# Norms by token tile, gains by row and whole first slabs in a two-block transformer on one core

## What is computed

```
h = rmsnorm(x, ln1);  z = h @ w_in                     # q, k, v of three attentions, three gates
merged = sum_b sigmoid(g_b) * (attention_b @ w_p_b);   x = x + merged @ w_o
h2 = rmsnorm(x, ln2); u = conv3(h2 @ w_up);            x = x + (silu(a) * b) @ w_down
x = rmsnorm(x, ln_f)
mem_n = rms_norm(mem, mem_norm_g);  kv = mem_n @ wkv   # 256 memory rows, 2048 columns
p = rms_norm(x, g0) @ w_in_first                       # convolution branch and RWKV branch
x = x + rms_norm(concat(conv, rwkv) @ w_out, g1)
x = x + rms_norm(cross_attention(rms_norm(x, g2) @ wq, kv) @ wo, g3)
x = x + rms_norm(swiglu(rms_norm(x, g4), w_gu, w_down), g5)

rmsnorm(x, g) = x * rsqrt(mean(x * x) + 1e-6) * g      # per token, g has 1024 entries
```

## Time and profile before

| | us |
|---|---|
| time, median of 3 runs | 938.48 (936.15 to 940.76) |
| profiled execution, its own time | 937.22 |
| its span in the trace | 935.0 |
| PE busy | 868.0 |
| DVE busy | 568.1 |
| ACT busy | 445.4 |
| POOL busy | 18.8 |
| bytes moved by DMA | 143.25 MB |

### The profile page before, as it was taken

How to read it: one execution, slowest core, us unless ns; L and a number is a source line. 1 busy time by engine, 2 the same in 40 slices (tenths; PEclk the granted TensorE clock), 3 DMA queues, 4 the chain that set the end, 5 groups by cost and what they waited for, 6 DMA issues and landing times.

```text
span 935.0 us, 18575 instructions
## 1 busy us (share of the span) xinstructions
PE 868.0 (93%) x7952; PEld 803.4 (86%) x7952; DVE 568.1 (61%) x686; ACT 445.4 (48%) x572; POOL 18.8 (2%) x26
## 2 busy tenths in 40 slices
PE   2999999997999999998998989999899699999996
PEld 1999989986999998887996979888797699999784
DVE  3375655575677776548579986566553645555434
ACT  5375655445555555535454411455554544444332
POOL 1100000000000000002000000000000000000000
PEclk9999999997999999998999999999999799999998
DMA  8743345444555555554443120234424255555531
GB/s 325 250 160 136 135 136 180 143 174 143 197 180 180 182 182 193 201 176 163 144 149 120 64 93 19 77 97 175 156 92 141 107 180 179 179 179 179 188 127 45
DMA packets 21100, 143.25 MB, mean 153 GB/s; under 512 B 2490, under 2 KB 2538, under 8 KB 4912
## 3 DMA queue, kind: packets, MB, share of 16 engines
q1 hardware_dynamic: 18720, 134.23, 42.0%
q0 software_dynamic: 2176, 7.27, 2.3%
q10 hardware_dynamic: 144, 0.85, 0.2%
HBM read 141.27 MB, written 1.07 MB: 152 GB/s over the span
## 4 chain that ended last, share of the span: by engine, by line
PE 80%; DVE 11%; ACT 5%; issue 2%; DMA 1%; SPq 0%; DVEq 0%; ACTq 0%
PE ps L1537 24%; PE ps L1539 23%; PE ps L1538 23%; DVE w_lo L893 4%; ACT w_hi L458 3%; PE ps L1891 2%; PE ps L1567 1%; PE ps L1841 1%; ACT xn L471 1%; DMA x<-in_x 1%; DVE xn L1437 1%; DVE x L1440 1%; PE ps L2058 1%; PE ps L2074 1%; DVE cacc L1206 1%
## 5 line engine op out<-in xcount | busy, mean ns | idle before, releaser
L893 DVE TENSOR_TENSOR w_lo<-raw,w_hi 128x2048 fp32r<-128x2048 f32 x126 | 289.6, 2299 | 198.3 <-ACT w_hi L458 198.3
L1537 PE MATMUL ps<-hT_hi,w_hi 128*128 128x256 f32 x1240 | 357.8, 289 | 3.7 <-DVE w_lo L893 3.7
L1538 PE MATMUL ps<-hT_lo,w_hi 128*128 128x256 f32 x1240 | 354.4, 286 | 0.0
L1539 PE MATMUL ps<-hT_hi,w_lo 128*128 128x256 f32 x1240 | 354.2, 286 | 0.0
L458 ACT ACTIVATE w_hi<-raw 128x2048 fp32r<-128x2048 f32 x126 | 240.9, 1912 | 172.0 <-PE ps L1539 171.2
L1537 PEld LDWEIGHTS ps<-hT_hi,w_hi 128*128 128x128 f32 x1240 | 242.0, 195 | 8.5 <-issue 7.3
L1538 PEld LDWEIGHTS ps<-hT_lo,w_hi 128*128 128x128 f32 x1240 | 241.8, 195 | 0.1
L1539 PEld LDWEIGHTS ps<-hT_hi,w_lo 128*128 128x128 f32 x1240 | 241.6, 195 | 0.0
L1539 PE MATMUL ps<-w_hi,gT_lo 128*128 128x512 f32 x176 | 70.1, 398 | 0.0
L1537 PE MATMUL ps<-w_hi,gT_hi 128*128 128x512 f32 x176 | 69.4, 394 | 0.1
L1538 PE MATMUL ps<-w_lo,gT_hi 128*128 128x512 f32 x176 | 69.4, 394 | 0.0
(11 more groups left out here) (277 smaller groups left out, 1040.2 us busy)
## 6 DMA issues: line engine op xcount, KB each, us to landing
raw<-in_weights SPq DMA_DIRECT2D x126, 1024.0 KB, 4.9
row_gain<-in_rows_vec POOLq DMA_DIRECT2D x4, 512.0 KB, 4.8
bias<-bias_scratch POOLq DMA_DIRECT2D x1, 1536.0 KB, 10.3
x<-in_x SPq DMA_DIRECT2D x2, 512.0 KB, 6.9
xn<-in_mem POOLq DMA_DIRECT2D x2, 512.0 KB, 4.2
out<-x SPq DMA_DIRECT2D x2, 512.0 KB, 2.6
masks<-in_masks ACTq DMA_DIRECT2D x1, 833.5 KB, 6.5
bias<-bias_scratch POOLq DMA_DIRECT2D x1, 768.0 KB, 11.9
```

Source lines behind the costliest of these rows:

```text
L893: V.tensor_tensor(w_lo[:, n % SPLIT, :], raw[:, n % RAW, :], w_hi[:, n % SPLIT, :].bitcast(F32), ALU.subtract).then_inc(sems["lo_ready"], 1)
L1537: mm(dst, left[0], right[0], start=first, stop=False)
L1538: mm(dst, left[0], right[1], start=False, stop=False)
L1539: return mm(dst, left[1], right[0], start=False, stop=last)
```

## The change

1. Leading norms. The gain is a row now (`norm_gain`, 128 copies of 1024 entries, loaded by DMA once per norm, the first on ACT's queue, the others on POOL's), and DVE multiplies x by root and gain in one instruction. PE transposes one token tile as soon as it is normed, into four banks; ACT and DVE fill `hT` in four pieces of 128 x 512 (token tile by half of the features).
2. First slabs. The first slab of qkv, up, wq and gu2 is multiplied whole, in two steps of waiting; the products wait for three of the four pieces, then for the fourth. At the start the split of slab 0 is done in two halves between the pieces.
3. The root's table. A dummy root on ACT (`root_table`) is issued ahead of six places.
4. Norms of products. DVE multiplies by the row gain as soon as the squares are summed, then does root and addition in one instruction. The last one is split in halves of 512 columns, each with its own output DMA. ACT writes its unused squares to PSUM there.
5. The start. x has one semaphore per tile; the weight loads wait for nothing; the masks come in a first part of 131 columns and the rest on POOL's queue; the row gain of ln_f is loaded later.
6. Around g0. ACT and DVE do the first norm ln_f tile by tile with the split of the second memory slab in between; the 16 transposes of g0 stand in the middle of that slab's products; the first slab of in2 waits for all of `hT`. Memory slabs stay 2, 5 and 1. POOL's tap matrices wait for the last `g_lo` of "up" rather than for the addition after "down".

```diff
-                sp.dma_start(x[:, t, :], x_in[0, t * P:(t + 1) * P, :]).then_inc(sems["x_in"], 16)
+                sp.dma_start(x[:, t, :], x_in[0, t * P:(t + 1) * P, :]).then_inc(sems[f"x_in_{t}"], 16)
             for n in range(RAW):
-                if n == 0:
-                    sp.wait_ge(sems["x_in"], 16 * TT)
-                if n == 1:
-                    sp.wait_ge(sems["masks_ready"], 16)
                 sp.dma_start(raw[:, n, :], weights[n]).then_inc(raw_in[n], 16)
...
+            pool.dma_start(masks[:, MASKS_FIRST:MASK_COLS], masks_in[:, MASKS_FIRST:MASK_COLS])\
+                .then_inc(sems["more_masks"], 16)
...
-            pool.wait_ge(sems["x_ready"], X_READY["down"] + TT)
+            pool.wait_ge(sems["g_lo_ready"], PAIRS)
...
-            act.dma_start(masks[:, 0:MASK_COLS], masks_in).then_inc(sems["masks_ready"], 16)
+            act.dma_start(masks[:, 0:MASKS_FIRST], masks_in[:, 0:MASKS_FIRST]).then_inc(sems["masks_ready"], 16)
+            act.dma_start(norm_gain[:, :], rows_in[4 + NORM_GAINS.index("ln1")].partition_broadcast(P))\
+                .then_inc(sems["first_gain"], 16)
...
+            def fill_part(name, t, half):
+                act.wait_ge(sems["xt_ready"], 4 * TRANSPOSED.index(name) + 2 * t + half + 1)
+                A(hT_hi[:, 4 * half:4 * half + 4, t * P:(t + 1) * P],
+                  bank(transposed_half(t, half)).rearrange("p (k n) -> p k n", k=4), ACT.Copy)\
+                    .then_inc(sems["hT_hi_ready"], 2)
...
+            def root_table(n):
+                A(stat[:, 61 + n % 2:62 + n % 2], stat[:, 60:61], ACT.Sqrt)
...
-            def normed(name, src=None):
+            def normed(name):
                 for t in range(TT):
-                    V.tensor_scalar(xn[:, t, :], (x if src is None else src)[:, t, :], inverse_rms(name, t), None,
-                                    ALU.mult).then_inc(sems["xn_ready"], 1)
...
+                    V.scalar_tensor_tensor(out=xn[:, t, :], in0=x[:, t, :], scalar=inverse, in1=norm_gain[:, :],
+                                           op0=ALU.mult, op1=ALU.mult).then_inc(sems["xn_ready"], 1)
...
-                    do(V.scalar_tensor_tensor(out=xn[:, t, :], in0=banks(4 + 2 * t, 2), scalar=inverse_rms(name, t),
-                                              in1=row_gain[:, :], op0=ALU.mult, op1=ALU.mult))
-                    settle()
-                    V.tensor_tensor(x[:, t, :], x[:, t, :], xn[:, t, :], ALU.add).then_inc(sems["x_ready"], 1)
+                    dve.wait_ge(sems["sumsq_ready"], TT * STATS[name] + t + 1)
+                    do(V.tensor_tensor(xn[:, t, :], banks(4 + 2 * t, 2), row_gain[:, :], ALU.mult))
...
+                        V.scalar_tensor_tensor(out=x[:, t, cols], in0=xn[:, t, cols], scalar=inverse, in1=x[:, t, cols],
+                                               op0=ALU.mult, op1=ALU.add).then_inc(sems["x_ready"], 1)
...
+            def transposes(name, t):
                 z = TRANSPOSED.index(name)
-                pe.wait_ge(sems["xn_ready"], TT * (z + 1))
+                pe.wait_ge(sems["xn_ready"], TT * z + t + 1)
+                for half in range(2):
+                    for k in range(4):
+                        last = nc.tensor.transpose(ps[:, transposed_half(t, half), k * P:(k + 1) * P],
+                                                   xn[:, t, (4 * half + k) * P:(4 * half + k + 1) * P], ident)
+                    last.then_inc(sems["xt_ready"], 1)
...
+            def memory_slabs(first, last, name):
+                for i in range(first, last):
+                    for j, _ in enumerate(memory_slab(i)):
+                        if name and i == last - 1 and j == 7:
+                            transposes(name, 0)
+                            transposes(name, 1)
```

More of the change, by code:

```diff
@@ L187, with transposed_half @@
 )
-def transposed_bank(name, k):
-    return k // 2 if name == "mem" else 2 + k // 2 % 2
+def transposed_half(t, half):
+    return 2 + 2 * t + half
 class Steps:
@@ L1693, in values @@
                     weighted_values(2 * g + pair)
-            for i in range(3):
+            for i in range(1, 3):
                 qkv_slab(i)
@@ L1750, in _, with feed_loop @@
             token_products("w_o", hT, lambda i: operand(FILL["merged"], 2 * i + 1))
-            transposes("ln2")
-            def feed_loop(name, fill):
+            def feed_loop(name, norm):
                 n0, u0 = FIRST_SLAB[name], FIRST_UNIT[name]
-                for j in range(2):
-                    used(features(n0 + j, u0 + j, fill if j == 0 else None))
+                first_slab(name, norm)
+                used(features(n0 + 1, u0 + 1, None))
                 with pe.Fori(0, (PAIRS - 1) // 2) as turn:
```

222 lines of the change are left out of this document (149 added, 73 removed).

## The result

The changed kernel takes 914.57 us (median of four runs, 914.4 to 915.84) against 938.09 (936.15 to 940.76): 0.9756 of the time before, with a 95% interval of 0.9739 to 0.9773. The forecast was 921.0 with a range of 916 to 927. So the direction was right and the gain too small by 6.4 us, outside the range. The profiled execution took 914.4 with a span of 912.6, before 937.22 with 935.0.

The account below looks back on a forecast made before the run. Bound: PE's matmuls plus 67 us in which PE has nothing. Terms for start, ln2, stage down, g0, g2, g4 and end summed to -17.25 us: 937.22 to 920.0, plus 1.3 for the median, 921; range 916 to 927.

Parts of the forecast that it names:

- The chains: Engine-by-engine waits at each norm: first products at 228.7 (ln2), 439.4 (g0), 661.3 (g2), 734.3 us (g4).
- the stall in stage down: Stage down: moved tap operations slow a split, so PE stalls once, costing 0.55 us, between 0 and 1.2.
- the last product to the end: Kernel's end: hidden table load, halved last tile and smaller DMA save 1.9 us, range 1.3 to 2.3.
- the clock's term at each seam: PE's clock behind each norm: gains of 0.4 at ln2, half of 1.5 at g0, 0.45 at g4; 0 to 1.3 lost at g2.
- rising some 6 us in: Start: slab 0's products run at the lower clock until it rises some 6 us in, as before.
- the sign set for a wrong forecast: After any seam: products at the lower clock for more than 5 us would show the forecast wrong.
- (a): Start stays bound by bytes, slab 0 lands at 14.1, one more seam at its lower bound: 924 us; chance 0.2.
- (b): Seams give less than the chains say, as the next wait takes over: -11.8, 926.5 us; chance 0.1.
- (c): Slower: short holes after seams keep PE's clock low; 50 us more of such products give 943 us; chance 0.02.
- (d): Change fails its purpose: table load returns before the root, or a later wait eats the gain; 934 us; chance 0.04.
- (e): Larger gain, -19 to -22, if slab 0 lands at 11 and the clock never falls at g0: 917.5 us; chance 0.1.
- What I had called free: Attention's bias tables: starting 1 us later relative to PE costs nothing, given an estimated 1.6 us of slack.

Follow-up runs that it names:

- a_g0_behind: Changed kernel with g0's 16 transposes behind the second memory slab instead of inside its products; 918.4 us, ratio 0.9803.
- b_pad544: Kernel before the change plus an unused 544-byte block per partition ahead of the masks, moving later tiles; 935.57 us, 0.9978 of the kernel before.
- a_bridge: Changed kernel with g2's transposes in the middle of memory slab 7 and ScalarE filling hT before copying that slab; 915.44 us, ratio 0.9769.
- a_bytes: Changed kernel with the start's old bytes restored (whole masks on ScalarE's queue, ln_f row gain at the start), order kept as changed; 919.89 us.
- a_no_dummy: Changed kernel without the six dummy roots; 919.83 us, ratio 0.9796.
- a_both: Changed kernel, but TensorE waits for both normed token tiles before transposing the first; 920.74 us, ratio 0.981.
- a_order: Changed kernel with the old order of first loads (x, then slab 0, then slab 1), bytes kept as changed; 918.07 us.
- a_warm2: Changed kernel with idle matmuls in TensorE's waits: 12 at ln2, 13 at g2, 23 at g4; 913.69 us, ratio 0.9732.
- a_bias: Changed kernel with the bias rows' matmuls ahead of slab 0 and ScalarE's copies of them ahead of slab 1's rounding; 913.96 us, ratio 0.9747.
- a_best2: a_bias plus a_warm2's idle matmuls, 13 more ahead of the first transposes and 5 ahead of the first product; 911.86 us, ratio 0.9724.
- a_taps: Changed kernel with GpSimd again building the tap matrices after the addition that follows stage down; 916.37 us, ratio 0.9782.
- a_warm: Changed kernel with 18 idle matmuls in TensorE's wait at ln2 and 38 at g4; 917.81 us, ratio 0.9789.
- a_best3: a_best2 with a_bridge's edit, which replaces the 13 idle matmuls at g2; 912.31 us, ratio 0.9732.

## Why the prediction came out wrong, point by point

**The chains were right.** In the frame of the kernel before (the changed kernel's time plus the lead over the kernel before with which it came to the norm) the first products start at 221.22 + 7.60 = 228.82 at ln2 (forecast 228.7), 427.87 + 11.26 = 439.13 at g0 (439.4), 645.03 + 15.98 = 661.01 at g2 (661.3), 718.38 + 15.89 = 734.27 at g4 (734.3). The hole at g0 is 1.61 (1.8), the stall in stage down 0.46 (0.55), slab 0 lands at 12.15 (11.9), the last product to the end takes 2.1 us less (1.9). No chain is off by more than 0.35 us. One account of them was wrong all the same: a_g0_behind shows that the place of g0's transposes moved no product.

**The step that failed is the clock's term at each seam.** I had written 0.4 us won at ln2, half of 1.5 at g0, 0.45 at g4, some 0.5 lost at g2 (661.3 by the chain, -0.7 in the sum) and "rising some 6 us in" at the start. What stands behind each first product is, ledger less chain: ln2 3.44 - 2.23 = 1.2 us gained, g0 4.33 - 2.81 = 1.5, g4 3.39 - 2.39 = 1.0, g2 0.1 + 1.45 = 1.6 lost. The start's first product came 8.0 us sooner (forecast 8.3) and 0.5 were lost behind it, where I had counted 1.9. Term by term, 1.1 + 0.6 + 1.1 + 0.6 - 0.8 (start, ln2, g0, g4, g2): 2.6 us more than the sum had. The rows of the clock bear this out by themselves: products at the lower level were 2.7, 3.5 and 2.3 us at ln2, g0 and g4 before and none after, and 1.4 before and 5.0 after at g2. At the 0.44 of my prices this is 1.2, 1.5 and 1.0 gained and 1.6 lost, as in the ledger. At the start it is 2.9 us where I had put 6, worth 1.4. The reason given for g2 (a wait of 3.5 in one piece) fits: the wait was 3.41. Its range held the outcome, but the loss passed the 1.3 that I had set as its bound, and the sign set for a wrong forecast, over 5 us of products at the lower level behind a seam, was just met there.

**Missing from the sum was the matmul's step in down and down2**, about 1.7 us in the ledger and 2.1 in b_pad544's median. It goes with the place of the tiles behind the block, though a_bridge shows that this is not the whole cause. No row of the kernel before could show it; the diff did show that tiles move.

**The rest**: 0.5 us in small drifts between the seams, 0.1 at the stall, 0.2 at the end, 0.4 outside the span (2.2 before, 1.8 after), and 1.1 of the 1.3 us that I added for the distance of the profiled execution to the median, which is 0.17 in the changed kernel. 2.6 + 1.7 + 0.5 + 0.1 + 0.2 + 0.4 + 1.1 = 6.6, of 6.7 that lie between 914.57 and the unrounded 921.2.

**The rivals.** (a) fell: slab 0 came at 12.15, though a_bytes shows that bytes do bind, and the 1.3 MB that I had set against it left the path only in part. (b) fell: ln2, g0 and g4 gave more than the chains said, and only g2 less. (c), slower by the clock, fell in sum but was right at g2, and it is what a_g0_behind, a_no_dummy and a_both suffer from: at ln2 a chain 1 us longer cost 2.5 and 3.1 us. (d) fell: no table load stands between squares and root at ln2 or the end, and TensorE's one new wait in stage down is 0.46. (e), the larger gain, is the one that came, beyond its far end and by half of its mechanism: the clock indeed never fell behind g0, slab 0 did not land at 11. That half was put there as a chance of 0.1 and not worked out from a row, so it was no foresight.

**What I had called free** was free only in the runs of the changed kernel: the bias tables' slack is used up, and later variants lose up to 1.4 us to it.

**Still open:** why the place of the tiles changes a matmul's step and why a_bridge has the slow step in one stage without any tile moved, and which waits bring the lower level in the RWKV stage. There, between 526 and 538 us, eight of the thirteen variants of the changed kernel (a_order, a_bytes, a_g0_behind, a_no_dummy, a_bridge, a_warm2, a_bias, a_best2) show the lower level, and the changed kernel itself does not, though none differs in that stage and the waits at its start, 1.80 and 0.91 us, are the same to a hundredth in the changed kernel, a_no_dummy and a_best2. I could not foresee such a phase from any row, and it is worth 1 to 2.5 us. Six variants (a_taps, a_g0_behind, a_warm, a_bridge, a_best2, a_best3) show the lower level for 3.4 us earlier in the stage too, between 474 and 484 us.

## What to carry to other kernels

Price a seam twice: the chain up to the first product, and then the products behind it at either clock level, with both values in the range; here the chains were good to 0.35 us, and each seam's clock moved by 1 to 1.6. When an edit pulls a stage forward, look up for every transfer needed there how long before its use it was issued, not whether it was ever waited for. And when buffers change place, the matmuls that read them can change by a per cent or two; test it with an unused block, and in both directions, before giving the gain to the edit.

## What the runs showed of the hardware that I had not expected

- A stage's slab took 5.50 or 5.60 us after nothing but a move of its tiles (blocks of 544 and 480 bytes), and in a_bridge 5.60 without one.
- Idle matmuls in waits are worth having only if they end before the data come: 12, 13 and 23 of 0.23 us each brought 3.5 us at three seams, of which 0.9 was left in the kernel's time; 18 and 38 lost 1.1 at two.
- VectorE's 128x2048 split took 2.29 us alone, 3.12 (changed kernel) and 4.01 (a_taps) beside GpSimd's two operations.
- A load of 2.3 MB beside the weight stream landed 13.4 us after its first issue in the changed kernel and 15.4 in a_warm2, from the same time of issue.
- The lower clock level does not follow from the waits alone: the same waits were followed by it in some kernels and not in others.
